# Latent attention: values scaled by token rows in place of probabilities, and the projections' place

## The chip, the cores and the metric

One core of one Trainium2 chip. The metric is the device time of one execution in microseconds, given as the median over runs.

## What is computed

The kernel runs a chain of transformer blocks over 512 tokens of width 1024, one after the other. The change touches one of them, the latent attention layer with 8 heads:

```python
def mla_layer(x, norm_g, w_in, q_a_norm, w_uq, kv_a_norm, w_ukv, q_head_norm, k_head_norm, w_out):
    ...
    q = (rms_norm(q_lat, q_a_norm) @ w_uq).reshape(B, S, MLA_HEADS, MLA_QK_DIM)
    kv = (rms_norm(kv_lat, kv_a_norm) @ w_ukv).reshape(B, S, MLA_HEADS, MLA_NOPE_DIM + MLA_V_DIM)
    k_nope, v = kv[..., :MLA_NOPE_DIM], kv[..., MLA_NOPE_DIM:]
    ...
    q = rms_norm(q, q_head_norm)
    k = rms_norm(k, k_head_norm)
    ...
    o = causal_softmax_attention(q, k, v, 1.0 / math.sqrt(MLA_QK_DIM)).reshape(B, S, MLA_WIDTH)
    return x + (o * jax.nn.silu(gate)) @ w_out
```

The softmax is causal: query block j of 128 tokens sees keys 0 to 128(j+1). A row's probabilities are exponentials divided by their sum, and the division can be made on the probabilities or on the row of the output.

## The kernel before

The program is written by hand as one instruction queue per engine, and each queue is executed in order. Semaphores tie them. TensorE (PE) multiplies into PSUM, ScalarE (ACT) and VectorE (DVE) read PSUM, GpSimd (POOL) makes the low halves of the weights (L284) from what ScalarE casts (L1050, `high`), and SyncE (SP) fetches the weight panels. Activations are feature-major: features on partitions, 512 tokens in the free dimension. An accurate product is three matmuls with high and low halves (L314 to L316, `exact3`).

The attention loop runs over v = 4h + j, head h = 0 to 7 and query block j = 0 to 3. Its steps:

- `mla_score(v+1)` on TensorE (L856 to L858), one step ahead, into bank 2 or 3.
- `mla_softmax` on VectorE: the row's maximum (L2350) and its negative, scaled (L2352).
- `mla_exp` on ScalarE (its instructions stand under L1044): exponentials into PB, their sum by row into COLS.
- `mla_scale` on VectorE: reciprocal (L2357) and PB times it (L2359).
- transposes of PB on TensorE (L899) into bank 4 or 5, ScalarE's copy into PT (L1598).
- `mla_values(v-1)` on TensorE (L867): values stationary, PT moving, so that the output has features on partitions. A head's four blocks fill bank 6 or 7.
- `mla_out` on VectorE: the finished head times its gate (L2363), split into high and low halves (L1783, L1785) for the output GEMM.

Beside this each step prepares later heads. `mla_proj` makes q, k, and the rope part of q two heads ahead, a tile each (L314 to L316). ScalarE squares each tile (L1044) and makes a scaled copy of q and k. `mla_rope` on VectorE (L2325, L2326) reads the rope tile and adds the squares up. `mla_sums` on TensorE (L835) adds the squares over features, `mla_root` on ScalarE takes the root, `mla_diag` on VectorE (L2332 to L2336) makes reciprocals and a diagonal matrix of them, `mla_spread` on TensorE (L843) turns that into rows over all partitions, and `mla_keys` on VectorE (L2342, L2343) scales the keys with it. `mla_score` of a head's first block waits for `mla_keys`.

All these products go through two PSUM banks, 0 and 1, handed out in turn by `take()`: a take waits until the bank's previous content has been released (`a_free`). `skip` on ScalarE and VectorE counts the takes that the other one reads. In a head the takes are sums, spread, q, k, rope.

## Time and profile before

| | |
|---|---|
| median of 3 runs | 2633.14 us (2630.51 to 2635.91) |
| profiled execution | 2636.3 us, its span 2634.2 us |
| PE busy, share of the span | 2480.3 us, 94% |
| DVE busy | 1342.9 us, 51% |
| ACT busy | 1024.2 us, 39% |
| POOL busy | 1009.3 us, 38% |
| granted clock of TensorE, mean | 0.97 |

The rest of the reading is on the 138 us of the attention loop, 5% of the span. The rows name engines PE, DVE, ACT, POOL; L and a number is a line of the kernel. A matmul on float32 operands stands as two records. Adjacent records of one line are merged in a timeline ("x4").

### The profile page before, as it was taken

To read this page: it belongs to the slowest core of one execution; us is meant where nothing else is said; L and a number is where in the kernel's file an instruction comes from. 1 tells how busy PE (TensorE), PEld (TensorE's weight loads), DVE (VectorE), ACT (ScalarE), POOL (GpSimd) and SP (SyncE) were. 2 spreads that over 40 slices of the span, in tenths; PEclk is the share of its full clock that TensorE was granted. 3 is DMA by queue.
4 is the path that set the end of the run, shared out by engine and by line. 5 is a ranking of instruction groups with operands and counts; after the bars stand their busy time and mean duration, and the time that the engine had idled before them with its cause. 6 is when DMAs were issued, how large, how long until landed. Compare 5 with 4: busy or idle time off the path is not lost.

```text
span 2634.2 us, 31252 instructions
## 1 busy us (share of the span) xinstructions
PE 2480.3 (94%) x11706; PEld 1988.1 (75%) x11706; DVE 1342.9 (51%) x1877; ACT 1024.2 (39%) x1327; POOL 1009.3 (38%) x758
## 2 busy tenths in 40 slices
PE   6999899899999899998998899999989998999999
PEld 5887677688887678766767678888869656688886
DVE  6456667866667661444447762222373544522224
ACT  5445576422222543665446442222243433322222
POOL 3332244445554443222443244444424104344442
PEclk8999999999999999999989999999989998999999
DMA  3221497222222122111221122222212102122221
GB/s 137 81 76 53 170 359 261 103 97 96 96 96 96 65 88 73 49 35 51 92 96 49 49 80 96 96 96 96 96 64 101 49 17 80 48 96 96 96 96 63
DMA packets 35813, 245.52 MB, mean 93 GB/s; under 512 B 3935, under 2 KB 3935, under 8 KB 7044
## 3 DMA queue, kind: packets, MB, share of 16 engines
q1 hardware_dynamic: 29952, 207.12, 22.1%
q10 hardware_dynamic: 5764, 37.06, 3.8%
q8 instruction: 66, 1.08, 0.2%
q14 instruction: 31, 0.25, 0.0%
HBM read 242.06 MB, written 2.11 MB: 93 GB/s over the span
## 4 chain that ended last, share of the span: by engine, by line
issue 55%; POOL 28%; PE 15%; DVE 1%; DVEq 0%; POOLq 0%; ACT 0%
POOL WL L284 28%; PE PS L314 5%; PE PS L316 5%; PE PS L315 5%; PE PS L1026 0%; PE PS L375 0%; DVE X L2421 0%; DVE ARENA L2416 0%; POOLq L288 0%; DVE ARENA L1764 0%; DVEq L2087 0%; DVEq L2420 0%; PE PS L380 0%; DVE ARENA L1739 0%; DVEq L1763 0%
## 5 line engine op out<-in xcount | busy, mean ns | idle before, releaser
L284 POOL TENSOR_TENSOR WL<-WT,WH 128x512 fp32r<-128x512 f32 x754 | 1009.1, 1370 | 1590.7 <-ACT WH L1050 1070.2
L314 PE MATMUL PS<-HH,WH 128*128 128x512 f32 x1568 | 624.9, 399 | 33.5 <-POOL WL L284 13.3
L315 PE MATMUL PS<-HL,WH 128*128 128x512 f32 x1568 | 616.7, 393 | 0.0
L316 PE MATMUL PS<-HH,WL 128*128 128x512 f32 x1568 | 616.5, 393 | 0.0
L1378 ACT CAST WH<-WT 128x2048 fp32r<-128x2048 f32 x90 | 172.1, 1912 | 605.5 <-PE PS L314 605.5
L314 PEld LDWEIGHTS PS<-HH,WH 128*128 128x128 f32 x1568 | 297.9, 190 | 113.6 <-POOL WL L284 15.0
L314 PE MATMUL PS<-YH,WH 128*128 128x512 f32 x840 | 333.8, 397 | 26.2 <-DVE ARENA L2343 7.0
L316 PEld LDWEIGHTS PS<-HH,WL 128*128 128x128 f32 x1568 | 298.0, 190 | 63.7
L315 PEld LDWEIGHTS PS<-HL,WH 128*128 128x128 f32 x1568 | 298.3, 190 | 59.5 <-issue 0.2
L315 PE MATMUL PS<-YL,WH 128*128 128x512 f32 x840 | 329.5, 392 | 0.0
L316 PE MATMUL PS<-YH,WL 128*128 128x512 f32 x840 | 329.4, 392 | 0.0
L1044 ACT ACTIVATE ARENA<-PS 128x512 f32<-128x512 f32 (+1 forms) x159 | 109.1, 691 | 351.7 <-PE PS L316 242.3
L1050 ACT CAST WH<-WT 128x2048 fp32r<-128x2048 f32 (+1 forms) x99 | 187.7, 1896 | 133.5 <-PE PS L314 102.9
L2118 DVE TENSOR_TENSOR ARENA<-PS,ARENA 128x512 f32<-128x512 f32 x44 | 30.4, 692 | 376.5 <-PE PS L316 376.5
L314 PEld LDWEIGHTS PS<-YH,WH 128*128 128x128 f32 x840 | 158.9, 189 | 70.8 <-DVE ARENA L2343 10.0
L1044 ACT ACTIVATE ARENA<-ARENA 128x512 f32<-128x512 f32 (+5 forms) x207 | 170.2, 835 | 100.4 <-DVEq L1780 26.9
L316 PEld LDWEIGHTS PS<-YH,WL 128*128 128x128 f32 x840 | 159.1, 189 | 33.6
L315 PEld LDWEIGHTS PS<-YL,WH 128*128 128x128 f32 x840 | 159.2, 190 | 31.3
L2146 DVE TENSOR_TENSOR ARENA<-PS,ARENA 128x512 f32<-128x512 f32 x176 | 121.3, 691 | 106.3 <-PE PS L316 104.4
L414 PE MATMUL PS<-HH,WH 128*128 128x512 f32 x240 | 102.0, 425 | 25.4 <-DVE HL L1751 19.2
L314 PE MATMUL PS<-WH,HH 128*128 128x256 f32 x384 | 112.1, 292 | 6.5 <-DVE HL L1773 4.4
L1044 ACT ACTIVATE ARENA<-PS,COLS 128x128 f32<-128x128 f32 (+3 forms) x102 | 57.5, 565 | 142.4 <-DVE COLS L2512 59.5
(305 smaller groups left out, 3370.0 us busy)
## 6 DMA issues: line engine op xcount, KB each, us to landing
WT<-weights SPq DMA_DIRECT2D x188, 1024.0 KB, 4.8
ARENA<-w_ada ACTq DMA_DIRECT2D x33, 1024.0 KB, 7.2
ARENA<-w_ada SPq DMA_DIRECT2D x3, 1024.0 KB, 7.7
X<-x_fm SPq DMA_DIRECT2D x4, 512.0 KB, 7.1
out_fm<-X SPq DMA_DIRECT2D x8, 256.0 KB, 2.1
ARENA<-rel_rows ACTq DMA_DIRECT2D x1, 1024.0 KB, 5.3
CON<-constants SPq DMA_DIRECT2D x1, 704.0 KB, 9.5
WT<-weights SPq DMA_DIRECT2D x1, 512.0 KB, 4.8
```

The lines of the kernel that those rows point to most:

```text
L284: i = nc.gpsimd.tensor_tensor(WL[s][:, e], WT[s][:, e], WH[s][:, e].bitcast(F32), ALU.subtract)
L314: i0 = nc.tensor.matmul(o, w[0], r[0], start=first, stop=False, skip_group_check=True)
L315: nc.tensor.matmul(o, w[0], r[1], start=False, stop=False, skip_group_check=True)
L316: i2 = nc.tensor.matmul(o, w[1], r[0], start=False, stop=last, skip_group_check=True)
L414: i0 = nc.tensor.matmul(psb(b), w[0], src[0][:, k, :], start=k == 0, stop=False, skip_group_check=True)
L1044: return nc.scalar.activation(o, i, fn, **kw)
L1050: nc.scalar.copy(WH[s][:, 0:width], WT[s][:, 0:width]).then_inc(sem("w_hi"), 1)
L1378: nc.scalar.copy(WH[s][:, :], WT[s][:, :]).then_inc(sem("w_hi"), 1)
L2118: free(tt(GT[:, q, :], psb(b), GE[:, q, :], ALU.mult), b)
L2146: tt(dst[:, j, :], psb(4 + j % 4), dst[:, j, :], ALU.add).then_inc(sem("b_read"), 1)
```

## The change

- `mla_scale` no longer touches the probabilities. The transposes wait for the exponential alone. `mla_values` has PT stationary and the values moving, so that the output has tokens on partitions; it alternates between banks 6 and 7 by v. `mla_scale` multiplies each 128x128 block of it by the reciprocal of the row's sum, from PSUM into the new tile OT, two steps after its block's turn in the loop.
- A new `mla_turn(h)` transposes the head's four blocks of OT into a bank that `take()` gives, at step j = 1 of the next head. `mla_out` reads that bank, at j = 2, and stands behind `mla_keys` on VectorE.
- q and k of two heads ahead are issued at the end of step j = 2, behind the values; the rope tile stays at j = 3. ScalarE reads q at the end of step 2, and k and rope in step 3. In a head the takes are now sums, spread, turn, q, k, rope.
- The working area grows by 448 columns; semaphore counts of the later forgetting attention are adapted.

```diff
--- before.py
+++ after.py
@@ -87,7 +87,7 @@
 FOX_STEPS = (0, 3, 6, 8, 10, 12, 14, 16)
 G_FFN3 = G_OUT4 + 4
 NPANEL = G_FFN3 + 3 * CH
-ARENA_N = 17472
+ARENA_N = 17920
 
 
 def build(nc, x_in, p_in, par_in, con_in, hot_in, rows_in, sguw_in, w_in, ada_in, rel_tmp, out, stage):
@@ -208,6 +208,7 @@
         QKT = [QKT0, a.tiles(4)]
         RK, KBASE = a(S), a(S)
         PB, PT = a.tiles(2), a.tiles(2)
+        OT = a.tiles(NQ, P)
         RQ = PB[:, 0, :]
 
         a = Carve()
@@ -861,13 +862,19 @@
             def mla_values(v):
                 h, j = divmod(v, NQ)
                 pe.wait_ge(sem("pt_ready"), v + 1)
-                if j == 0 and h >= 2:
-                    pe.wait_ge(sem("mlo_read"), h - 1)
+                if v >= 2:
+                    pe.wait_ge(sem("on_ready"), v - 1)
                 for kb in range(j + 1):
-                    m = nc.tensor.matmul(PS[:, 6 + h % 2, P * j:P * (j + 1)], LV[:, kb, P * h:P * (h + 1)], PT[:, v % 2, P * kb:P * (kb + 1)],
+                    m = nc.tensor.matmul(PS[:, 6 + v % 2, P * j:P * (j + 1)], PT[:, v % 2, P * kb:P * (kb + 1)], LV[:, kb, P * h:P * (h + 1)],
                                          start=kb == 0, stop=kb == j, skip_group_check=True)
-                if j == NQ - 1:
-                    m.then_inc(sem("o_ready"), 1)
+                m.then_inc(sem("mo_ready"), 1)
+
+            def mla_turn(h):
+                b = take()
+                pe.wait_ge(sem("on_ready"), NQ * (h + 1))
+                for t in range(NQ):
+                    m = nc.tensor.transpose(PS[:, b, P * t:P * (t + 1)], OT[:, t, :], IDENT)
+                m.then_inc(sem("a_done"), 1)
 
             pe.wait_ge(sem("lat_ready"), 1)
             mla_proj(0, False)
@@ -890,9 +897,9 @@
                     mla_sums(h + 1)
                 if j == 1 and h + 1 < MLA_HEADS:
                     mla_spread(h + 1)
-                if j >= 2 and h + 2 < MLA_HEADS:
-                    mla_proj(h + 2, j == 3)
-                pe.wait_ge(sem("pn_ready"), v + 1)
+                if j == 3 and h + 2 < MLA_HEADS:
+                    mla_proj(h + 2, True)
+                pe.wait_ge(sem("pe_exp"), v + 1)
                 if v >= 2:
                     pe.wait_ge(sem("pt_ready"), v - 1)
                 for kb in range(j + 1):
@@ -900,7 +907,12 @@
                 m.then_inc(sem("ptr_ready"), 1)
                 if v:
                     mla_values(v - 1)
+                if j == 1 and h:
+                    mla_turn(h - 1)
+                if j == 2 and h + 2 < MLA_HEADS:
+                    mla_proj(h + 2, False)
             mla_values(n["att"] - 1)
+            mla_turn(MLA_HEADS - 1)
             out_gemm(G_OUT3, (YH, YL), "mly_ready")
 
 
@@ -1001,7 +1013,7 @@
                             open_panel(G_OUT4)
                         ob[e] = take()
                     out_step(G_OUT4, (YH, YL), "gy_ready", P * e, ob[e], k)
-                pe.wait_ge(sem("pn_ready"), n["att"] + v + 1)
+                pe.wait_ge(sem("pn_ready"), v + 1)
                 pe.wait_ge(sem("pt_ready"), n["att"] + v - 1)
                 for kb in range(j + 1):
                     m = nc.tensor.transpose(PS[:, 4 + v % 2, P * kb:P * (kb + 1)], PB_[:, v % 2, P * kb:P * (kb + 1)], IDENT)
@@ -1582,22 +1594,21 @@
             mla_exp(0)
             for v in range(n["att"]):
                 h, j = divmod(v, NQ)
-                if j == 2 and h + 2 < MLA_HEADS:
-                    mla_proj(h + 2, "q")
-                if j == 1 and h + 1 < MLA_HEADS:
-                    skip(1)
+                if j == 1:
+                    skip((h + 1 < MLA_HEADS) + (h > 0))
                 if v + 1 < n["att"]:
                     mla_exp(v + 1)
                 if j == 0 and h + 1 < MLA_HEADS:
                     mla_root(h + 1)
-                if j == 2 and h + 2 < MLA_HEADS:
-                    mla_proj(h + 2, "k")
                 if j == 3 and h + 2 < MLA_HEADS:
-                    mla_proj(h + 2, "r")
+                    mla_proj(h + 2, "kr")
                 act.wait_ge(sem("ptr_ready"), v + 1)
                 nc.scalar.copy(PT[:, v % 2, 0:P * (j + 1)], PS[:, 4 + v % 2, 0:P * (j + 1)]).then_inc(sem("pt_ready"), 1)
+                if j == 2 and h + 2 < MLA_HEADS:
+                    mla_proj(h + 2, "q")
                 if j == 3 and h + 2 < MLA_HEADS:
                     next_panel(mlh(h + 2))
+            skip(1)
             out_gemm(G_OUT3, lambda k: MOD[:, 8 + k:9 + k])
 
 
@@ -2353,14 +2364,14 @@
 
             def mla_scale(v):
                 h, j = divmod(v, NQ)
-                dve.wait_ge(sem("pe_exp"), v + 1)
+                dve.wait_ge(sem("mo_ready"), v + 1)
                 nc.vector.reciprocal(COLS[:, 4 + j:5 + j], COLS[:, j:j + 1])
                 dve.drain()
-                ts(PB[:, v % 2, 0:P * (j + 1)], PB[:, v % 2, 0:P * (j + 1)], COLS[:, 4 + j:5 + j], None, ALU.mult).then_inc(sem("pn_ready"), 1)
+                ts(OT[:, j, :], PS[:, 6 + v % 2, P * j:P * (j + 1)], COLS[:, 4 + j:5 + j], None, ALU.mult).then_inc(sem("on_ready"), 1)
 
             def mla_out(h):
-                dve.wait_ge(sem("o_ready"), h + 1)
-                tt(LG[:, h, :], psb(6 + h % 2), LG[:, h, :], ALU.mult).then_inc(sem("mlo_read"), 1)
+                b = take()
+                free(tt(LG[:, h, :], psb(b), LG[:, h, :], ALU.mult), b)
                 dve.drain()
                 split(LG[:, h, :], h, "mly_ready")
 
@@ -2373,22 +2384,24 @@
             skip(2)
             mla_rope(1)
             mla_softmax(0)
-            mla_scale(0)
             for v in range(NQ * MLA_HEADS):
                 h, j = divmod(v, NQ)
                 if v + 1 < NQ * MLA_HEADS:
                     mla_softmax(v + 1)
-                    if j == 1 and h:
-                        mla_out(h - 1)
-                    if j == 2 and h + 1 < MLA_HEADS:
-                        mla_keys(h + 1)
-                    mla_scale(v + 1)
+                if j == 2 and h + 1 < MLA_HEADS:
+                    mla_keys(h + 1)
+                if j == 2 and h:
+                    mla_out(h - 1)
+                if v >= 2:
+                    mla_scale(v - 2)
                 if j == 0 and h + 1 < MLA_HEADS:
                     mla_diag(h + 1)
                 if j == 2 and h + 2 < MLA_HEADS:
                     skip(2)
                 if j == 3 and h + 2 < MLA_HEADS:
                     mla_rope(h + 2)
+            mla_scale(NQ * MLA_HEADS - 2)
+            mla_scale(NQ * MLA_HEADS - 1)
             mla_out(MLA_HEADS - 1)
             n["att"] = NQ * MLA_HEADS
             dve.drain()
@@ -2516,7 +2529,7 @@
                 ts(PB_[:, v % 2, 0:P * (j + 1)], PB_[:, v % 2, 0:P * (j + 1)], COLS[:, 4 + j:5 + j], None, ALU.mult).then_inc(sem("pn_ready"), 1)
 
             def fox_out(p):
-                dve.wait_ge(sem("o_ready"), MLA_HEADS + 2 * p + 2)
+                dve.wait_ge(sem("o_ready"), 2 * p + 2)
                 nc.vector.tensor_copy(YB[:, p, :], psb(6 + p % 2)).then_inc(sem("fo_read"), 1)
 
             def gate_root(q):
```

## Rows read from the trace of the kernel before

**Rows 1.** Windows by stage: us, busy PE, PEld, DVE, ACT, POOL, clock, DMA

```profile
1368.80:1507.00 138.20, 119.80 (x659) 95.11 (x658) 96.52 (x198) 82.94 (x155) 35.08 (x26) 0.91 0.15 54
```

**Rows 2.** Timeline, PE, head 3: start, us, engine, line, names [idle before <-releaser]

```profile
1420.44 0.51 PE L314 MATMUL PS<-YH,WH 128*128 128x512 f32 x1 [0.87 <-DVE ARENA L2343]
...
1422.02 0.39 PE L856 MATMUL PS<-ARENA 128*128 128x128 f32 x2
...
1422.53 0.45 PE L314 MATMUL PS<-YH,WH 128*128 128x512 f32 x1
...
1423.97 0.60 PE L899 MATMUL PS<-CON,ARENA 128*128 128x128 f32 x4
...
1426.89 1.92 PE L835 MATMUL PS<-CON,ARENA 128*128 128x1 f32 x16 [0.72 <-DVE ARENA L2326]
...
1431.58 1.13 PE L843 MATMUL PS<-ARENA,CON 128*128 128x128 f32 x8 [0.36 <-DVE ARENA L2334]
...
1432.99 1.02 PE L856 MATMUL PS<-ARENA 128*128 128x512 f32 x2
...
1434.77 0.45 PE L314 MATMUL PS<-YH,WH 128*128 128x512 f32 x1
...
1438.17 0.50 PE L314 MATMUL PS<-YH,WH 128*128 128x512 f32 x1 [1.80 <-DVE ARENA L2343]
```

**Rows 3.** Timeline of the same head, ACT

```profile
1423.35 0.46 ACT L1044 ACTIVATE ARENA<-PS,COLS 128x128 f32<-128x128 f32 x1 [0.36 <-DVE COLS L2352]
...
1424.17 0.60 ACT L1044 ACTIVATE ARENA<-PS 128x512 f32<-128x512 f32 x1 [0.27 <-PE PS L316]
...
1425.13 1.91 ACT L1050 CAST WH<-WT 128x2048 fp32r<-128x2048 f32 x1
...
1436.41 0.60 ACT L1044 ACTIVATE ARENA<-PS 128x512 f32<-128x512 f32 x1 [1.84 <-PE PS L316]
...
1437.47 0.78 ACT L1044 ACTIVATE ARENA<-PS,COLS 128x512 f32<-128x512 f32 x1
```

**Rows 4.** Timeline of the same head, DVE

```profile
1422.73 0.29 DVE L2350 TENSOR_REDUCE COLS<-PS 128x1 f32<-128x128 f32 x1 [0.42 <-PE PS L858]
...
1424.87 0.75 DVE L2325 SCALAR_TENSOR_TENSOR ARENA<-PS,PAR,CON 128x512 f32<-128x512 f32 x1 [0.41 <-ACT ARENA L1044]
...
1428.33 1.43 DVE L2359 TENSOR_SCALAR ARENA<-ARENA,COLS 128x256 f32<-128x256 f32 x1
...
1429.98 1.45 DVE L2334 TENSOR_TENSOR ARENA<-CON,COLS 128x512 f32<-128x512 f32 x1
...
1431.36 1.23 DVE L2336 TENSOR_SCALAR COLS<-COLS 128x4 f32<-128x4 f32 x1
...
1432.66 0.56 DVE L2350 TENSOR_REDUCE COLS<-PS 128x1 f32<-128x384 f32 x1
...
1433.42 0.68 DVE L2363 TENSOR_TENSOR ARENA<-PS,ARENA 128x512 f32<-128x512 f32 x1
...
1435.95 0.68 DVE L2350 TENSOR_REDUCE COLS<-PS 128x1 f32<-128x512 f32 x1
```

**Rows 5.** Timeline of the same head, POOL

```profile
1427.12 5.45 POOL L284 TENSOR_TENSOR WL<-WT,WH 128x512 fp32r<-128x512 f32 x4 [12.45 <-ACT WH L1050]
```

**Rows 6.** Windows of 2 us, head 1; the last 0.50 is the clock

```profile
1394.00:1396.00 2.00, 2.00 (x6) 1.38 (x6) 1.93 (x3) 1.49 (x2) 2.00 (x2) 0.50 0.00 0
```

**Rows 7.** Timeline, PE: after keys 2, after keys 7, the output GEMM

```profile
1402.56 0.50 PE L314 MATMUL PS<-YH,WH 128*128 128x512 f32 x1 [0.88 <-DVE ARENA L2343]
...
1491.96 0.49 PE L856 MATMUL PS<-ARENA 128*128 128x128 f32 x2 [1.40 <-DVEq L2344]
...
1507.00 0.48 PE L314 MATMUL PS<-YH,WH 128*128 128x512 f32 x1
```

**Rows 8.** What L899 (transposes) waited for, whole kernel: us, times

```profile
  DVE ARENA L2359: 7.0, 6
```

**Rows 9.** Lines of the loop: the scales, xcount | busy us, mean ns | idle

```profile
L2359 DVE TENSOR_SCALAR ARENA<-ARENA,COLS 128x128 f32<-128x128 f32 (+3 forms) x32 | 18.8, 588 | 2.5
```

## Prediction

> **What bounds the kernel now.** First the windows by stage. The latent attention's loop runs from 1368.8 to 1507.0 us; TensorE is busy for 119.8 of its 138.2 us, VectorE for 96.5, ScalarE for 82.9 [rows 1]. No engine is full, so what counts is who hands over to whom. Next the timeline of one head. I write S(3,1) for the scores of head 3, token block 1 (T and V for its transposes and values), and count time from the moment at which `mla_keys` of a head ends on VectorE and lets TensorE go on: 1420.44 us for head 3, 1438.17 for head 4 [rows 2]. Period: 17.73 us. From head 2 (1402.56) to head 7 (1491.96, a score that waits for the same thing) it is 89.4 us, 17.9 each [rows 7].
>
> TensorE waits ahead of `mla_sums(4)` (1426.89, 6.45 after the keys), whose inputs need head 4's rope; a little ahead of `mla_spread(4)` (1431.58); and 1.80 us ahead of the k tile of head 5, whose PSUM bank `mla_keys` still reads (1438.17) [rows 2]. VectorE runs without a pause from the diag (1429.98) to the keys' end: two held instructions (1.45 and 1.23), softmax, `mla_out` of head 2, a scale, softmax, keys [rows 4]. So the loop is: keys, k tile and S(3,0), ScalarE's exponential and squares, VectorE's rope, sums, root, diag, VectorE's run, keys.
>
> **The change, part by part.** *The scale leaves the path between exponential and transpose.* TensorE waited for it 6 times, 7.0 us in all [rows 8], and none of these waits is in the head shown: in the steady heads this gives nothing. VectorE's work falls. The 32 scales took 18.8 us [rows 9]; the new ones read 128 columns of PSUM each. I price one at 0.29 us, by the nearest instruction that reads 128 PSUM columns (the reduce at 1422.73) [rows 4], and take 0.24 for reciprocal and drain; bounds for the pair 0.4 and 0.8. The 256-column scale took 1.43 us while GpSimd ran (1427.12 to 1432.57) [rows 4, 5]. It ends just as the diag's input arrives, so its going frees nothing. The diag's own two instructions stay held: ScalarE's cast, which starts GpSimd, moves with them.
>
> A rule bears on this place. The row shows an SBUF-only scale of 256 columns held to 1.43 us beside GpSimd, where the mean of all 32 is 0.59 [rows 4, 9]. The Trainium skill (GPSIMD Engine Reference, Key points) says that GpSimd shares its SBUF interfaces with VectorE instructions that take two SBUF inputs or run in a two-port mode. By it the new scale, which reads PSUM, would escape the hold; that speaks for the change, and on the path it would be worth 1.1 us a head. By the row's place it lies beside the path and is worth nothing.
>
> *Four transposes and their wait.* `mla_turn` costs TensorE 0.45 us (four transposes of this shape show 0.60 with the last one's tail) [rows 2]. It sits ahead of S(3,3) and waits for the scale of block (2,3), which on VectorE stands behind the diag and softmax(3,2). From the diag's end (1431.36 + 1.23 = 1432.59) to the next keys' end it was 5.58. After: softmax(3,2) 0.83 with hand-over (1432.66 to 1433.42), scale 0.53, hand-over 0.1, turn 0.45: S(3,3) at 1.9. Its reduce can begin 1.98 later (S(3,3) to the next tile, 1432.99 to 1434.77, and 0.2 for the matmul's tail), and from that reduce to the keys' end it is 2.22 (1435.95 to 1438.17) [rows 2, 4]. Sum 6.1. `mla_out` and a scale (2.53 together, 1433.42 to 1435.95) have left this stretch, but the scores stand in it instead: **+0.6 a head** (bounds 0.4 and 0.9, by the scale's). Queued behind the waiting turn are S(3,3) and T(3,2); VectorE waits for that score with nothing else to do.
>
> *The projections.* With turn between spread and q, q no longer gets the bank that the root frees early (it started at 1434.77, before the keys' end) but spread's, which only `mla_keys` frees; k gets turn's, freed by the first instruction of `mla_out`, 0.7 later and in time. From the keys' end: q tile 0 to 1.44 (as the rope tile, 1422.53 to 1423.97); ScalarE's two reads of q 1.64 to 2.70 (1434.77 to 1436.41, and 1436.41 to 1437.47); k tile to 2.25 (half of q's and a hand-over); S(3,0) at 2.25, where it stood at 1.58; its reduce 2.96 (0.71 later), exponential 3.58 (0.62 later), over at 4.15. Only then, in ScalarE's new order, the two reads of k to 5.2, where the rope's square followed at once before (1424.17, that is 3.7). VectorE's rope at 5.9 (0.70 later), sums at 7.9 (2.02 later) [rows 2 to 4]. Before: 6.45. **+1.5 a head**, less 0.1, since GpSimd is no longer delayed by the 256-column scale and releases the diag sooner (bounds 0 and 0.25). `mla_out` and a scale (2.53 again) end 2.6 after the keys, before the reduce at 2.96, and are hidden; with less cover they would push it by up to 0.6. From sums to the diag's end all keeps its distance, the cast 0.96 behind the square included [rows 3]; the panel's fetch on SP follows GpSimd and has over ten us to spare.
>
> *Ends.* Head 2's q still gets the early bank (there is no turn before block (1,1)), so the first period pays the second loss alone, 0.5. From the last keys to the output GEMM it was 15.1 us (1491.96 to 1507.00) [rows 7]. After: two transposes near the end lose their wait for a scale (part of the 7.0), but V(7,2) waits for the scale of (7,0), which stands behind `mla_out` of head 6 (2.0), and behind V(7,3) come a scale 0.53, the turn 0.45 and hand-overs. Followed step by step it comes to 16.6: **+1.5**, bounds -0.5 and +3.
>
> **Sum.** Five periods (keys 2 to keys 7) x 2.0 = 10.0, first period 0.5, end 1.5: +12.0. TensorE idles some 5 us a head instead of 3.4, and already now its granted clock is 0.50 (1.2 GHz) for some 4 us of about half of the heads, mostly beside the path [rows 6]; I add 1. On the profiled execution's 2636.3 us (span 2634.2 and 2.1 around it) this gives 2649.3; the median of the runs is 3.2 below that execution, so **2646**. The forecast's own range is 2641 to 2651.
>
> **The rivals.**
> 1. *The lower clock lands on the path.* The new waits stand right ahead of q, k and S(3,0) (2.7 us of TensorE) and of turn and S(3,3) (2.2); one of the groups runs at 1.2 GHz. Against: full speed followed the wait of 1.80 at 1438. Price 2.2 x 6 heads = 13: 2659. Chance 0.18.
> 2. *Faster: VectorE's load is what binds.* If the waits close up, a period follows VectorE's work, and that falls from 18.8 us of scales to 32 x 0.29 = 9.3: 2624. For: VectorE has no gap in the 8.2 us before the keys' end. Against: the in-order queues above. It decides if TensorE waits no more than 0.9 ahead of sums and under 0.6 ahead of the turn. Chance 0.13. The Trainium skill's rule above would put half of that gain down to the hold.
> 3. *q doesn't wait for the keys,* or ScalarE's new order absorbs it. Then 0.6 x 6 + 1.5 = 5 is left: 2638, or less if the end costs nothing. Chance 0.14.
> 4. *The turn finds its input early.* VectorE's stretch then loses 2.5 and gains 0.5, against 1.4 for the projections: -0.6 x 6 and +1.5 at the end: 2631. Chance 0.05.
>
> The forecast has 0.50. A measurement can tell about 0.2% (5.3 us) from no change. Slower by more: the forecast, rival 1 and a part of rival 3, 0.74; within: 0.13; faster: 0.13. The range from 2630 to 2660 leaves out rival 2 and the far end of rival 1.
>
> **What would show it.** Between two keys' ends there should be about 19.8 us. TensorE should start the q tile just after the keys, wait some 1.5 us ahead of L835 and about 1 us ahead of the new transposes, released by the new scale; that scale should be near 0.29 us and never over 1. The loop should last some 150 us. I am wrong if sums start less than 7 us after the keys, if the new transposes don't wait, or if the diag is no longer held.

## The result and the profile after

| | before | after |
|---|---|---|
| median | 2633.82 us, 4 runs (2630.51 to 2635.91) | 2653.35 us, 4 runs (2648.60 to 2657.00) |
| profiled execution, its span | 2636.3, 2634.2 us | 2652.43, 2650.4 us |
| loop, 1368.8 us to the output GEMM | 138.2 us | 158.2 us |
| TensorE busy in the loop | 119.8 us | 129.2 us |
| VectorE busy in the loop | 96.5 us | 87.4 us |
| TensorE at 1.2 GHz, keys of head 1 to the output GEMM, summed over windows of 1 us | 17.1 us | 27.3 us |

The ratio is 1.0073 (95% interval 1.0061 to 1.0085): slower by 19.5 us in the medians, where 12.9 were forecast. VectorE has 9.1 us less to do, and the loop is 20.0 us longer. In the row for the loop, which answers to [rows 1], the columns are again us, busy PE, PEld, DVE, ACT, POOL, the granted clock and the DMA's share; the first line below it is the group of the new scales (it answers to [rows 9]), the second what the transposes of the turn waited for.

```profile
1368.80:1526.95 158.15, 129.15 (x691) 103.12 (x690) 87.42 (x198) 82.48 (x155) 34.78 (x26) 0.89 0.14 47
...
L2370 DVE TENSOR_SCALAR ARENA<-PS,COLS 128x128 f32<-128x128 f32 x32 | 11.2, 351 | 2.5
...
  DVE ARENA L2370: 4.9, 5
```

Of these 20.0 us, 3.8 are given back later, where nothing was changed: two stretches (1571 to 1607 and 1925 to 1959 us) have TensorE's lower clock for shorter and end 1.8 and 2.0 us sooner. The spans differ by 16.2.

The timeline of head 2 in the kernel after, from its keys' end (1404.94) to that of head 3 (1424.63), all at full clock. (Head 3, which [rows 2] show, has the lower clock here.) TensorE first:

```profile
1405.09 0.47 PE L315 MATMUL PS<-YH,WH 128*128 128x512 f32 x1 [1.59 <-DVE ARENA L2354]
...
1407.24 0.38 PE L857 MATMUL PS<-ARENA 128*128 128x128 f32 x2
...
1412.79 1.92 PE L836 MATMUL PS<-CON,ARENA 128*128 128x1 f32 x16 [1.12 <-DVE ARENA L2337]
...
1420.01 0.63 PE L876 MATMUL PS<-CON,ARENA 128*128 128x128 f32 x4 [1.00 <-DVE ARENA L2370]
1420.48 1.02 PE L857 MATMUL PS<-ARENA 128*128 128x512 f32 x2
```

Then ScalarE and VectorE:

```profile
1409.02 0.59 ACT L1056 ACTIVATE ARENA<-PS 128x512 f32<-128x512 f32 x1
1409.50 0.69 ACT L1056 ACTIVATE ARENA<-PS,PAR 128x512 f32<-128x512 f32 x1
1410.06 0.60 ACT L1056 ACTIVATE ARENA<-PS 128x512 f32<-128x512 f32 x1
...
1410.77 0.75 DVE L2336 SCALAR_TENSOR_TENSOR ARENA<-PS,PAR,CON 128x512 f32<-128x512 f32 x1 [1.74 <-ACT ARENA L1056]
...
1413.42 0.35 DVE L2370 TENSOR_SCALAR ARENA<-PS,COLS 128x128 f32<-128x128 f32 x1
...
1415.88 1.40 DVE L2345 TENSOR_TENSOR ARENA<-CON,COLS 128x512 f32<-128x512 f32 x1
...
1417.21 1.23 DVE L2347 TENSOR_SCALAR COLS<-COLS 128x4 f32<-128x4 f32 x1
...
1418.51 0.56 DVE L2361 TENSOR_REDUCE COLS<-PS 128x1 f32<-128x384 f32 x1
...
1419.51 0.35 DVE L2370 TENSOR_SCALAR ARENA<-PS,COLS 128x128 f32<-128x128 f32 x1
...
1422.46 0.69 DVE L2361 TENSOR_REDUCE COLS<-PS 128x1 f32<-128x512 f32 x1 [2.60 <-PE PS L859]
```

Read it as a round. TensorE stands 1.59 us for the keys, since q's bank is now the spread's (1405.09). S(2,0) follows at 1407.24, 2.30 behind the keys, where it stood 1.58 behind them. ScalarE reads k (two instructions) before the rope tile, so VectorE's rope starts at 1410.77, and the sums at 1412.79, 7.85 after the keys' end on VectorE. Counted the same way it was 6.50 before; the 6.45 of the prediction counts from TensorE's start, 0.05 later. Behind the diag comes softmax (1418.51), the scale (1419.51), only then the turn, which TensorE had waited 1.00 for, and behind it the scores of block 3. VectorE idles 2.60 us for those (1422.46). The keys end 6.19 after the diag.

### The profile page after: what moved, and what is told of

It is laid out like the page before. It is cut to its first block, busy times and chain, and to the rows that moved or that the text cites. A ratio compares the mean times of both kernels' runs of the same rounds, so it can differ in the third digit from the quotient of the medians.

```text
span 2650.4 us, 31348 instructions
## 1 busy us (share of the span) xinstructions
PE 2484.8 (94%) x11738; PEld 1993.0 (75%) x11738; DVE 1333.6 (50%) x1877; ACT 1023.7 (39%) x1327; POOL 1009.4 (38%) x758
## 4 chain that ended last, share of the span: by engine, by line
issue 55%; POOL 28%; PE 15%; DVE 1%; DVEq 0%; POOLq 0%; ACT 0%
POOL WL L285 28%; PE PS L315 5%; PE PS L316 5%; PE PS L317 5%; PE PS L1038 0%; PE PS L376 0%; DVE X L2434 0%; DVE ARENA L2429 0%; POOLq L289 0%; DVE ARENA L1775 0%; DVEq L2098 0%; DVEq L2433 0%; PE PS L381 0%; DVE ARENA L1750 0%; DVEq L1774 0%
```

## Result in detail: where the half clock stands

In two of the five later heads (3 and 5) another 1.6 us are lost. Below, head 3, from 1424.63 to 1445.92: windows of 1 us with TensorE alone (us, busy, granted clock, DMA), then its rows.

```profile
1433.00:1434.00 1.00, 1.00 (x9) 0.74 0.00 0
1434.00:1435.00 1.00, 1.00 (x7) 0.50 0.00 0
...
1439.00:1440.00 1.00, 1.00 (x5) 0.50 0.79 139
1440.00:1441.00 1.00, 1.00 (x10) 0.84 0.92 385
```

```profile
1436.88 1.23 DVE L2347 TENSOR_SCALAR COLS<-COLS 128x4 f32<-128x4 f32 x1
1436.89 1.49 PE L857 MATMUL PS<-ARENA 128*128 128x384 f32 x2
...
1439.80 0.56 DVE L2361 TENSOR_REDUCE COLS<-PS 128x1 f32<-128x384 f32 x1 [1.70 <-PE PS L859]
```

The clock was 1.2 GHz from about 1433.5 to 1440.3, 6.8 us. Before it fell, TensorE had stood 1.14 us ahead of the sums (1432.46) and then run the sums, 16 matmuls of one column in 2.6 us. The scores of block 2 take 1.49 us each where they take 0.81 at full clock (1415.61 in the head before), and VectorE, whose diag was over at 1438.11, waits 1.70 us for them. So the half clock is not on the scores of block 3, as my first rival had it, but a block earlier, and there it reaches the path.

The kernel before has the same fall in half of its heads, but shorter. This is its head 1 [rows 6], windows of 1 us and VectorE's softmax:

```profile
1393.00:1394.00 1.00, 1.00 (x8) 0.68 0.00 0
1394.00:1395.00 1.00, 1.00 (x4) 0.50 0.00 0
...
1396.00:1397.00 1.00, 1.00 (x4) 0.62 0.00 0
```

```profile
1391.08 1.92 PE L835 MATMUL PS<-CON,ARENA 128*128 128x1 f32 x16 [0.72 <-DVE ARENA L2326]
...
1397.12 0.56 DVE L2350 TENSOR_REDUCE COLS<-PS 128x1 f32<-128x384 f32 x1 [0.35 <-PE PS L858]
```

It is 3.4 us at 1.2 GHz (1393.4 to 1396.8) instead of 6.8. The fall comes 2.3 us behind the start of the sums, in the kernel after 1.0 behind it, and the softmax is 0.35 late instead of 1.70.

In heads 1 to 6 of the kernels without fills every stretch at 1.2 GHz is either 3.4 or 6.8 us long: 6.8 where it began 0.3 to 1.3 us behind the start of the sums (14 times), 3.4 where it began 1.4 or more behind it. The wait ahead of the sums doesn't decide the length: with the placeholder of the second experiment it is 1.12, and three stretches of 3.4 us follow. The tail, from the keys of head 7 on, has its own: 3.4 us in the kernel before (from 1492.35) and 6.8 in the kernel after (from 1508.6).

## The experiments

I compare the kernels by four stretches in the profiled execution, each between ends of instructions on VectorE or starts on TensorE: keys' end to the start of the sums; sums to the diag's end; diag's end to the next keys' end; and the tail, from the keys of head 7 to the output GEMM. The first three are taken from the five periods between the keys of head 2 and of head 7, in us. "Full" are heads that keep the full clock throughout, "fall" those with a stretch at 1.2 GHz; the tail's own time at 1.2 GHz stands behind it. A ratio is to runs of the kernel before on the same chip, whose medians were 2633.8 to 2636.0:

| kernel | keys to sums | diag to keys, full | diag to keys, fall | tail (at 1.2 GHz) | GEMM starts | median, us | ratio to before (95%) |
|---|---|---|---|---|---|---|---|
| before | 6.50 | 5.5 | 5.7 to 6.0 | 15.1 (3.4) | 1507.0 | 2633.8 | |
| after | 7.85 | 6.19 | 7.8 | 20.3 (6.8) | 1527.0 | 2653.4 | 1.0073 (1.0061 to 1.0085) |
| move alone | 6.4 | none | 5.7 to 6.0, 7.3 | 15.4 (3.4) | 1511.2 | 2640.0 | 1.0015 (1.0005 to 1.0025) |
| move and a placeholder | 7.85 | 5.46 | 6.1 | 13.8 (0) | 1513.5 | 2643.2 | 1.0030 (1.0018 to 1.0042) |
| turn a block later | 7.85 | 4.56 | 5.7, 7.4 | 16.0 (0) | 1511.5 | 2639.8 | 1.0013 (1.0002 to 1.0023) |
| the same, own bank | 7.4 | none | 7.37 | 15.9 (0) | 1518.5 | 2647.6 | 1.0044 (1.0028 to 1.0061) |
| the same, old projections | 8.4 | 4.56 | 5.7, 7.3 | 15.9 (0) | 1519.0 | 2644.4 | 1.0040 (1.0027 to 1.0054) |
| scale ahead of `mla_out` | 7.85 | 6.19 | 6.2, 7.8 | 17.0 (0) | 1521.8 | 2649.5 | 1.0051 (1.0034 to 1.0068) |
| after, with fills | 7.75 | 6.13 | 6.8 | 17.3 (0) | 1519.6 | 2649.0 | 1.0056 (1.0039 to 1.0072) |
| before, with fills | 6.4 | 5.5 to 5.7 | none | 13.7 (0) | 1498.7 | 2631.3 | 0.9989 (0.9980 to 0.9999) |
| spread out | 6.06 | 5.63 | 5.63 | 17.5 (3.4) | 1504.6 | 2635.7 | 1.0007 (0.9997 to 1.0017) |
| spread out, fills | 7.1 | 5.63 | none | 15.8 (0) | 1503.4 | 2634.8 | 1.0005 (0.9995 to 1.0014) |
| spread further | 6.08 | 4.77 (once) | 6.45 | 17.5 (3.4) | 1500.5 | 2633.2 | 0.9999 (0.9987 to 1.0010) |
| the same, fills | 5.97 | 5.46 | 7.08 | 16.5 (0) | 1503.1 | 2636.8 | 1.0008 (0.9999 to 1.0017) |

Sums to the diag's end is 5.70 in before and 5.63 to 5.79 in the others, but for the four kernels at the end of the table. The kernels end the keys of head 0 at 1360.0 to 1366.3 us, a difference that arises in earlier, unchanged stretches; so the start of the GEMM is to be read beside the stretches, not alone. Where a stretch of 1.2 GHz falls differs between kernels, so a tail or a head is best compared with one of the same clock.

### The move of the projections alone

The kernel before, with q and k of two heads ahead behind the values and in ScalarE's order of after; no turn, the old scales.

```diff
-                if j >= 2 and h + 2 < MLA_HEADS:
-                    mla_proj(h + 2, j == 3)
+                if j == 3 and h + 2 < MLA_HEADS:
+                    mla_proj(h + 2, True)
...
                 if v:
                     mla_values(v - 1)
+                if j == 2 and h + 2 < MLA_HEADS:
+                    mla_proj(h + 2, False)
```

> Edit: the kernel before with the projections' move alone (q and k at the end of block 2 behind the values, rope tile at block 3, ScalarE's new reading order); probabilities are scaled as before, there is no turn, so q keeps the bank that the root frees early. My theory (the loss of the move comes from q waiting for the keys' bank, which needs the turn's take): q starts ahead of the keys' end, sums start 6.6 us after it instead of 6.45, period 17.9, time 2635 (2632 to 2638). Rival (the move itself costs the 1.5 us a head, by ScalarE reading k only after the exponential): sums 7.5 or more after the keys' end, period near 19, time 2641 or more.

Measured: 2639.99 us, which is above the expected range. Sums start 6.40 to 6.46 after the keys, and the six periods from the keys of head 1 on are 17.8 to 18.1 in four heads and 19.45 in two. Between keys and sums the place of the projections and ScalarE's new order cost nothing: q still gets the early bank. The two long heads have the half clock for 6.8 us, which the expectation had left out. Windows of 1 us of TensorE, and the rows of one of them:

```profile
1427.41 2.58 PE L835 MATMUL PS<-CON,ARENA 128*128 128x1 f32 x16 [1.14 <-DVE ARENA L2326]
...
1431.81 1.49 PE L856 MATMUL PS<-ARENA 128*128 128x384 f32 x2
...
1434.72 0.56 DVE L2350 TENSOR_REDUCE COLS<-PS 128x1 f32<-128x384 f32 x1 [1.61 <-PE PS L858]
```

```profile
1428.00:1429.00 1.00, 1.00 (x9) 0.74 0.00 0
...
1434.00:1435.00 1.00, 1.00 (x4) 0.50 0.77 131
```

q and k no longer stand ahead of T and V, so the wait ahead of the sums is 1.14 instead of 0.72, though the sums start no later. The clock falls 1.1 behind the start of the sums and is down for 6.8 us, twice as long as in the kernel before; in four other heads of this run it is down for 3.4. That the move brings the longer stretches is seen here and argued, not shown.

### The same with a placeholder for the turn

```diff
+            def mla_dummy():
+                b = take()
+                for t in range(NQ):
+                    m = nc.tensor.transpose(PS[:, b, P * t:P * (t + 1)], IDENT, IDENT)
+                m.then_inc(sem("a_done"), 1)
...
+                if j == 1 and h:
+                    mla_dummy()
```

> The move of the projections alone (the first experiment) plus one placeholder: four transposes of the identity into a bank taken between the spread and the q tile, freed by a one-column copy on VectorE right behind mla_keys. No output is touched, the values stay as before, nothing waits for the placeholder's input. If it is the order of the banks that costs the 1.5 us between keys and sums, q now waits for the keys in every head from head 3 on, sums start 7.3 to 7.9 us after the keys where they started 6.4, and a period is 19.2 to 19.4 at full clock: about 2645 to 2648 us. If the bank is not the cause (the changed order on ScalarE, or the turn's wait itself), sums stay at 6.4 to 6.5 and the time at 2640.

```profile
1421.95 0.47 PE L314 MATMUL PS<-YH,WH 128*128 128x512 f32 x1 [1.18 <-DVE ARENA L2351]
...
1429.66 2.20 PE L835 MATMUL PS<-CON,ARENA 128*128 128x1 f32 x16 [1.12 <-DVE ARENA L2334]
```

Measured: 2643.17 us, 2 below what was expected. q waits for the keys (L2351 is their second instruction), and sums start 7.82 to 7.85 after them in all five periods from head 2 on, against 6.40 to 6.46 without the placeholder. Nothing waits for the placeholder's data: **the one take between spread and q is what costs the 1.4 us.** Its own four transposes and the one-column copy that frees the bank show in no other stretch: diag to keys at full clock is 5.46, as before. The periods are 19.0 twice and 19.65 three times, in place of 19.2 to 19.4; the three have 3.4 us of half clock behind the sums.

### The turn a block later

The kernel after, with `mla_turn(h - 1)` at step j = 2, behind the values and ahead of the projections.

```diff
-                if j == 1 and h:
+                if j == 2 and h:
                     mla_turn(h - 1)
```

> Edit: the changed kernel with the turn of the previous head one block later, behind the scores (h,3) and the values of block 1, ahead of q; the order of the banks stays. My theory (the turn waits for a scale behind the diag and holds up the scores): the wait ahead of the turn goes, and from the diag's end to the keys' end it is 4.6 us instead of 6.1, so a full-speed period is 18.2 instead of 19.7 and the time some 10 us below the changed kernel, 2643 (2640 to 2648). Rival (the turn's wait only takes the place of waits that come anyway): period 19.5 or more, time as the changed kernel, 2653.

```profile
1416.10 0.61 PE L868 MATMUL PS<-ARENA 128*128 128x128 f32 x4
1416.54 0.60 PE L876 MATMUL PS<-CON,ARENA 128*128 128x128 f32 x4
```

Measured: 2639.81 us, just below the expected range. TensorE goes from the values (L868) to the turn (L876) without a wait. Keys to sums stays at 7.85, since the turn is still the take between spread and q. Diag to keys is 4.56 at full clock, against 6.19: the scores of block 3 no longer stand behind the turn's wait. Heads at full clock have a period of 18.06. So both terms stand alone: 1.6 for the turn's place, 1.4 for the bank. As a whole it is 0.13% slower than before (0.02 to 0.23); one head takes 20.85.

### Its own bank for the turn

The turn a block later and in bank 5, which the transposes of block 3 then wait for; q's bank is the early one again.

```diff
-                b = take()
                 pe.wait_ge(sem("on_ready"), NQ * (h + 1))
                 for t in range(NQ):
-                    m = nc.tensor.transpose(PS[:, b, P * t:P * (t + 1)], OT[:, t, :], IDENT)
-                m.then_inc(sem("a_done"), 1)
+                    m = nc.tensor.transpose(PS[:, 5, P * t:P * (t + 1)], OT[:, t, :], IDENT)
+                m.then_inc(sem("mtb_ready"), 1)
```

> Edit: as turn_late, and the turn writes the transposes' bank 5, which is free at that point, instead of taking one of the two shared banks (transposes of block 3 wait until the gate has read it). So q gets the early bank again. My theory now: q starts before the keys' end, but VectorE's gate multiplication and a scale (2.6 us after the keys) stand ahead of the next softmax, so sums start 7.5 us after the keys instead of 7.8: a small gain over turn_late, 2641 (2637 to 2645). Rival (the bank is the whole of the 1.5 us): sums at 6.5 after the keys, time near 2634.

Rows behind the keys of head 4, which end at 1441.40:

```profile
1441.54 0.69 DVE L2374 TENSOR_TENSOR ARENA<-PS,ARENA 128x512 f32<-128x512 f32 x1
...
1442.32 0.38 PE L857 MATMUL PS<-ARENA 128*128 128x128 f32 x2
...
1443.73 0.35 DVE L2370 TENSOR_SCALAR ARENA<-PS,COLS 128x128 f32<-128x128 f32 x1
1444.00 0.28 DVE L2361 TENSOR_REDUCE COLS<-PS 128x1 f32<-128x128 f32 x1
```

Measured: 2647.55 us, above the expected range. The scores of block 0 stand at 0.92 after the keys, and their maximum is taken only at 2.60, where it stood at 1.56 to 1.62 with the move alone: `mla_out`, its split and a scale are ahead of it on VectorE. That work was hidden only because the bank was late; with the bank right it takes over 1.0 of the 1.4, and sums start at 7.4. Of the five periods every one has 6.8 us of half clock, with the scores of block 2 in it, and a diag to keys of 7.37. So this kernel is 7.7 us slower than the last, though its sums come 0.5 sooner after the keys; the wait ahead of them is 2.0 instead of 1.1.

### The same with the projections at their old place

Here only the scaling by rows and the turn are left of the change (bank 5, turn at j = 2); q and k are back ahead of the transposes of block 2, as in before.

```diff
-                if j == 3 and h + 2 < MLA_HEADS:
-                    mla_proj(h + 2, True)
+                if j >= 2 and h + 2 < MLA_HEADS:
+                    mla_proj(h + 2, j == 3)
```

> The scaling by rows and the turn, but with the projections where they were before, the turn in a bank of its own and placed behind the values of block 1. The front then has q early, as before. Expected by the walk: the gate's multiplication on VectorE waits for the turn, which now stands behind the k tile (about 1.9 us after the keys), it and its split and a scale end at about 4.6, so the next softmax is some 2.2 us late and sums start 8.6 after the keys; from diag to keys 4.6, as with the late turn. Period 18.9, about +1.1 a head, some 2641 us. If the rows are free once the projections stay, the period is 17.7 or less and the time 2634 or less.

```profile
1425.55 0.69 DVE L2374 TENSOR_TENSOR ARENA<-PS,ARENA 128x512 f32<-128x512 f32 x1 [2.28 <-PE PS L875]
...
1427.94 0.28 DVE L2361 TENSOR_REDUCE COLS<-PS 128x1 f32<-128x128 f32 x1
...
1431.71 3.22 PE L836 MATMUL PS<-CON,ARENA 128*128 128x1 f32 x16 [1.71 <-DVE ARENA L2337]
```

Measured: 2644.40 us, sums 8.43 to 8.50 after the keys (8.6 expected), 4.56 from diag to keys at full clock, one period of 18.62 and the others of 19.8 to 21.4; the time is 3.4 above the 2641 expected, since the half clock was left out of the sum. The gate waits 2.28 for the turn, which stands behind q's and k's tiles, and softmax of block 0 waits behind the gate. The rows alone are not free either, and the move of the projections, whose cost in the change is the bank's, has a use: it lets the turn come ahead of them.

### The scale ahead of `mla_out`

```diff
-                if j == 2 and h:
-                    mla_out(h - 1)
                 if v >= 2:
                     mla_scale(v - 2)
+                if j == 2 and h:
+                    mla_out(h - 1)
```

> Edit: the changed kernel with VectorE's scale ahead of the gate multiplication in block 2 (two lines swapped). My theory (part of the loss after the last keys is values that wait for a scale behind the gate multiplication of an older head): the waits of the values for the scale, 1.43 and 0.92 us, go; steady periods stay at 19.7; from the last keys to the output GEMM 18 us instead of 20.3, time 2651 (2648 to 2654). Rival (the end is lost to the lower clock and to the turn alone): 20 us and 2653 as before.

Measured: 2649.48 us. The periods stay (19.67 at full clock), and the tail is 17.0 instead of 20.3. The time and the tail agree with my theory, but most of the gain has another cause. First the tail of the kernel after (TensorE, all behind the keys of head 7):

```profile
1509.40 1.62 PE L868 MATMUL PS<-ARENA 128*128 128x128 f32 x6 [1.43 <-DVE ARENA L2370]
...
1518.03 0.63 PE L876 MATMUL PS<-CON,ARENA 128*128 128x128 f32 x4 [1.09 <-DVE ARENA L2370]
...
1523.99 1.80 PE L868 MATMUL PS<-ARENA 128*128 128x128 f32 x14 [0.92 <-DVE ARENA L2370]
...
1526.95 0.48 PE L315 MATMUL PS<-YH,WH 128*128 128x512 f32 x1
```

The first wait, V(6,2) for the scale of (6,0), is gone with the scale first. In its place the transposes of block 1 wait 0.80 for ScalarE's exponential, whose softmax stands behind `mla_out` on VectorE in both orders:

```profile
1508.51 0.33 PE L906 MATMUL PS<-CON,ARENA 128*128 128x128 f32 x1 [0.80 <-ACT ARENA L1056]
```

And this tail is all at full clock, where that of the kernel after has 6.8 us at 1.2 GHz. The run that tells the two apart is the next one: the kernel after with fills keeps the order of the kernel after, and its V(6,2) waits the same 1.43, but its tail too is at full clock. It takes 17.3. So of the 3.3 us the new order is worth 0.3 and the clock 3.0. Whether the order also moved the stretch of 1.2 GHz out of the tail is open: with the scale first it lies in head 6 instead, from 1492.55.

In earlier heads q, k and the rope tile fill the place behind the keys on TensorE and cover `mla_out`; in the last two heads there are none.

### Fills against the half clock

Matmuls of 512 columns that compute nothing, where TensorE waits: in the kernel before three ahead of the sums and six ahead of the k tile; in the kernel after four ahead of the sums, three ahead of the turn, six ahead of q.

```diff
                 b = take()
+                if h:
+                    keep_warm(psb(b), 3)
                 pe.wait_ge(sem("hc_ready"), h + 1)
```

> Edit: the kernel before with such matmuls in its two waits, 3 ahead of the sums and 6 between the q and the k tile. Theory: its periods of 17.7 to 18.2 become 17.7, since its half clock lay mostly beside the path; time 2633 (2631 to 2636). Rival (the lower clock costs the kernel before as much as the changed one): 1.6 us in each of four heads, 2628 or less.

> Edit: the changed kernel with matmuls whose result nobody reads in three of TensorE's waits: 4 ahead of the sums (bank already taken), 3 ahead of the turn, 6 ahead of the q tile (into scores' bank 2), each 512 columns of float32r, 0.23 us. Theory (besides the two hand-overs the lower clock on the path costs 1.6 us in the heads that it hits): no half clock in the loop, every period 19.7, keys 1 to keys 7 118 us instead of 121.6, end 19 instead of 20.3, time 2648 (2645 to 2651). Rival (the lower clock lies beside the path, and 21.3 instead of 19.7 has another cause): half clock gone and two periods still 21.3, time 2653.

In the kernel before the half clock is gone from the loop, 0 us instead of 17.1; the period falls from 17.9 to 17.7 and the tail from 15.1 to 13.7. Its ratio of 0.9989 (0.9980 to 0.9999) is the only one here below 1 with its whole interval, by a tenth of a percent. In the kernel after 13.6 us of half clock are left of 27.3, none of it in the tail, which falls from 20.3 to 17.3. Only one of its periods is 19.6, the other four are 20.3: in head 4 the clock falls at 1451.3, behind the sums, and the fills ahead of the turn then push it by half a microsecond. The time is as expected, the account of it only in part.

```profile
1451.00:1452.00 1.00, 1.00 (x8) 0.65 0.00 0
1452.00:1453.00 1.00, 1.00 (x5) 0.50 0.00 0
```

Here no wait came ahead of the fall: TensorE's busy time is 0.93 to 1.00 of each window from 1442 on, with the 16 one-column matmuls in it. Waits are thus not the whole cause, and what decides between the heads stays open.

### Versions meant to beat the kernel before

Own bank, turn a block later, the reciprocals apart from the scales, k's tile read ahead of the exponential, and VectorE's work (gate, low half, scales) spread over blocks 2, 3 and 0. The diff is between the first and the third of them, where less of it stands ahead of the softmax of block 1; the second is the first, the fourth the third, with fills.

```diff
                 if j == 2:
                     mla_recip(v - 2)
                 if j == 3 and h:
                     mla_gate(h - 1)
                 if j == 3:
                     mla_mult(v - 3)
+                    mla_recip(v - 2)
                 if j == 3 and h + 2 < MLA_HEADS:
                     mla_rope(h + 2)
-                if j == 3 and h:
-                    mla_low(h - 1)
+                if j == 0 and h:
+                    mla_mult(v - 3)
+                if j == 0 and h >= 2:
+                    mla_low(h - 2)
```

> Edit: own_bank, and three moves that follow from the walk: VectorE's gate multiplication of the older head goes behind the softmax of the next head's first block, its low half behind the rope; ScalarE reads k ahead of that block's exponential, rope behind it. Theory (hand-overs bind, and they can be taken out): sums start 5.7 us after the keys' end instead of 7.36, from the diag's end to the keys' end 4.6 at full clock, so the period is 15.9 at full clock and 17.5 where the half clock hits; time 2625 to 2635. Rival (VectorE's load binds): the period doesn't fall below 17.

> Edit: tuned, with 3 such matmuls ahead of the sums and 4 between the q and the k tile. Theory: no half clock in the loop, each period 15.9, time 2623 (2619 to 2628), below the kernel before. Rival (the fills stand in the way or don't hold the clock): as tuned or slower.

> The version with its own bank and VectorE's pieces spread out (tuned), further cut: ahead of the rope stands only the gate, one scale and one reciprocal, and the low half and two scales go behind the softmax of block 1. In tuned that softmax came 1.1 us late (VectorE still worked on the low half and a scale), and with it the exponential, the root behind it and the diag. If that is what holds tuned at 17.75 a head, the period falls to 16.6 and the time by 6 x 1.1 us to about 2628, that is 0.998 of before. If the half clock or the waits on ScalarE hold it, the period stays at 17.7 and the time at 2635.

> tuned2 with filling matmuls (512 columns of the identity's row, 0.24 us each at 2.4 GHz) at the place where its clock falls: one ahead of the sums, inside TensorE's wait of 0.51 us there, and three ahead of the transposes of block 0, right behind the sums. In tuned2 the scores of block 2 behind them take 1.49 us each at 1.2 GHz and the next softmax on VectorE ends up 1.1 us behind the diag. At full clock those scores would end 0.8 us before the diag does, so three fills (0.7 us) have cover. If the fills hold the clock, diag to keys falls from 6.45 to 5.6 and the period from 17.45 to 16.6, about 2628 us. If they don't hold it, they only push (up to 0.7 a head) and the time is 2633 to 2638.

The first three came out above the time expected of them, the last where its rival put it. Spread out, sums come to 6.06 after the keys, but a period is 17.75 where some 16 were expected, with the half clock and without it: a low half and a scale push softmax and exponential of block 1, and with them the table load that the root stands behind, 1.1 us. With fills it has no half clock in the loop, yet they stand in the way: keys to the diag's end is 12.8 us for 12.1. The kernel spread further takes the 1.1 us away: keys to the diag's end falls from 12.1 to 11.0, as expected. Its period is 17.45 all the same, since the half clock now reaches the path. VectorE waits 1.11 us for the scores of block 2 at 1.2 GHz:

```profile
1424.12 1.49 PE L857 MATMUL PS<-ARENA 128*128 128x384 f32 x2
...
1426.99 0.56 DVE L2363 TENSOR_REDUCE COLS<-PS 128x1 f32<-128x384 f32 x1 [1.11 <-PE PS L859]
```

With four fills around the sums three heads run at full clock and take 16.46, 1.2 less than a head at full clock in the kernel before; two others fall to 1.2 GHz behind the fills and take 18.05. The fills have a price of their own: the one period without them that ran at full clock took 15.79, 0.67 less (TensorE's rows and a window of 1 us):

```profile
1425.25 1.27 PE L463 MATMUL PS<-CONR 128*128 128x512 f32 x3
...
1426.00:1427.00 1.00, 1.00 (x6) 0.50 0.00 0
```

Medians of 2633.2 and 2636.8 against 2636.0 and 2635.4 of before on the same chips. Neither is measurably faster.

## Why the prediction was right, and where its sizes were off

The sign, the two hand-overs and the steady head at full clock were right. The time of 2646 was 7.4 short of 2653.35: inside the stated range, but outside the forecast's own range of 2641 to 2651, and nearer to rival 1's 2659. It came that near with some luck, since 3.8 us of the loop's loss are given back in unchanged stretches; in the loop itself 13.0 were forecast and 19.95 measured. Point by point, in the profiled execution. The start of the output GEMM moved by 19.95: 0.5 before the keys of head 1, 1.9 in the first period, 12.35 in the five periods, 5.2 in the tail.

- **The scale leaves the path: nothing.** As said. The new scales take 0.35 each (0.29 taken), 11.2 in all against 18.8 [rows 9]. That VectorE works 9 us less in the loop shortened nothing, as every stretch ends with a hand-over.
- **The hold.** The scale at 1413.42 lies inside GpSimd's 5.40 us (1413.02) and takes 0.35, where the old one at the same place took 1.43 [rows 4, 5]; the diag's two, at 1.40 and 1.23, stay held. The Trainium skill's rule (GPSIMD Engine Reference, Key points), by which GpSimd is in the way of two SBUF inputs and two-port modes, agrees with the scale that reads PSUM and with the diag's first instruction, which has two SBUF inputs. In which mode the diag's second one (128x4) and the old scale run, no row shows. As forecast the escape was worth nothing at this place.
- **The bank: +1.5 a head.** 7.85 from keys to sums for 7.9, that is 1.35 more than before; the placeholder shows the bank as the cause and 1.4 as its price. The wait ahead of the sums is 1.12 for 1.5.
- **The turn: +0.6 a head.** Diag to keys 6.19 for 6.1, the wait 1.00 for 1. Against the mean of before, 5.67 (its own half clock in it), 0.5. Turned a block later, the stretch is 4.56.
- **The period at full clock** was to be 19.8 and is 19.69. Sums to the diag's end is 0.05 shorter of the 0.1 taken; GpSimd starts at the same distance from the sums (0.23) and runs 5.40 instead of 5.45.
- **The clock: +1 in all.** This is the term that was mis-sized most. It cost 1.6 in each of two heads, 1.4 in the first period (1.9 for 0.5; with the scale first, where this head has 3.4 us of half clock instead of 6.8, the period is 1.4 shorter) and, in the tail, 3.0 against the 1.4 that it cost there before: some 6 in all. I had read the half clock of before as beside the path, which it mostly was; here it lasts 6.8 us instead of 3.4 and reaches the scores of block 2. Rival 1 had the mechanism, at the wrong scores (block 3 instead of block 2), for all heads instead of two of five, and at a price of 13.
- **The end: +1.5, bounds -0.5 and +3.** It was +5.2. Tails at full clock take the clock out of this: 13.7 in the kernel before with fills, 17.3 in the kernel after with fills. So the walk of the end was short by 2 us (+3.6 for +1.5), and the other 1.6 are the clock's, as said. I had kept the cover of the steady head, q, k and the rope tile, for the last heads, where there are no projections: `mla_out` of head 5 stands ahead of the scale that V(6,2) waits 1.43 for, and ahead of the softmax of S(7,0). Putting the scale first gains only 0.3 of it. Then the turn of head 6 waits 1.09 for its scale, which my walk left out too. S(7,3) starts 8.9 after the keys, in the kernel before with fills 5.8.

Rivals 2 and 4 fell: sums wait 1.12 or more, and the turn waits. Rival 3 fell too: q waited 1.59 for the keys. Where q had the early bank beside the turn (own bank), sums still came 7.4 after the keys, by VectorE's `mla_out`.

By the stretches, keys to sums cost 6.7 of the 12.35, diag to keys at full clock 2.6, the half clock in two heads 3.3, less 0.3 between sums and the diag's end.

## What to carry to other kernels

Where buffers are handed out in turn, an operation that takes one moves every later taker to another buffer, and so to another wait: follow the ring, and test it with a placeholder that does next to nothing else. Work that leaves one engine's path helps only if the hand-over behind it comes sooner; here less work for VectorE met a new wait on TensorE in each head. Walk the last rounds of a loop apart from the steady one, since what covers a wait there may have run out. And before a shorter stretch is put down to an edit, compare the granted clock in both: the swap of two lines seemed to be worth 3.3 us, and 3.0 of them were the clock's.

## What the runs showed of the hardware

- In the steady heads the granted clock falls to 1.2 GHz behind the start of the sums, 16 matmuls of one column each that take 1.9 us, and it does so in some heads and not in others of one execution, with nearly the same rows before it: a head with 1.12 us of wait ahead of the sums (1412.79) keeps 1.00 throughout, the next with 1.14 (1432.46) falls.
- What 3.4 us at 1.2 GHz cost depends on what lies in them: nothing in the kernel spread out (5.63 from diag to keys with and without), 0.65 a head with the placeholder (6.1 for 5.46), 1.2 with the turn a block later (5.75 for 4.56).
- Fills took the half clock out of the loop of two kernels altogether (before, and spread out) and left half of it in a third (after); in the fourth it cost 1.6 us in each head where it fell.
- Beside GpSimd an instruction of VectorE on 128x4 elements takes 1.23 us (1417.21), where it takes 0.16 without GpSimd, while a scale that reads PSUM takes its usual 0.35. The rows show until when it is held: until the instruction of GpSimd that is under way ends. GpSimd's (in the kernel after) ends at 1418.41 and the one of VectorE at 1418.44; it is so, to 0.03, in every head of the kernels before, after and spread further. The diag's first instruction (128x512) ends 0.55 behind the end of GpSimd's and takes GpSimd's next one from 1.27 to 1.7. In the kernel spread further it starts 0.07 before GpSimd's instruction ends, and takes its usual 0.69:

```profile
1416.68 1.73 POOL L285 TENSOR_TENSOR WL<-WT,WH 128x512 fp32r<-128x512 f32 x1
...
1424.03 0.69 DVE L2347 TENSOR_TENSOR ARENA<-CON,COLS 128x512 f32<-128x512 f32 x1
1424.07 1.78 POOL L285 TENSOR_TENSOR WL<-WT,WH 128x512 fp32r<-128x512 f32 x1
```

The first line is of the kernel after, the other two of the kernel spread further. A subtraction of two 128x512 tiles in SBUF took 1.21 beside GpSimd and 0.69 elsewhere (same kernel).
